# Level masks ahead on GpSimd, product copies on ScalarE, and one add for X and its transpose in the triangular inverse of an RWKV-7 mixer

## What is computed

```python
def wkv_scan(state0, r, kk, v, decay, b, k, reverse):
    def step(S, inp):
        r_t, kk_t, v_t, w_t, b_t, k_t = inp
        sa = jnp.einsum('bhvk,bhk->bhv', S, kk_t)
        S = S * w_t[:, :, None, :] - sa[..., None] * b_t[:, :, None, :] + v_t[..., None] * k_t[:, :, None, :]
        return S, jnp.einsum('bhvk,bhk->bhv', S, r_t)
    xs = tuple(jnp.moveaxis(t, 1, 0) for t in (r, kk, v, decay, b, k))
    S, ys = lax.scan(step, state0, xs, reverse=reverse)
    return S, jnp.moveaxis(ys, 0, 1)

def rwkv_mixer(z_lat, z_ctx, p, need_ctx):
    ...
    for d in range(2):
        reverse = d == 1
        s_ctx, yc = wkv_scan(s0, cx[0], cx[1], cx[2], *cx[4][d], reverse)
        _, yl = wkv_scan(s_ctx, lat[0], lat[1], lat[2], *lat[4][d], reverse)
```

## Time and profile before

| | us |
|---|---|
| median of 3 runs | 2557.57 (2556.31 to 2559.59) |
| the profiled execution, its time | 2553.7 |
| its span | 2551.6 |
| PE busy over the span | 2080.0 (82%) |
| DVE busy | 862.8 (34%) |
| POOL (GpSimd) busy | 377.2 (15%) |
| ACT (ScalarE) busy | 357.1 (14%) |

### The profile page before, as it was taken

The page is one execution under the profiler, slowest core; times in us unless marked ns, Lnnn a source line. Parts: engine busy times, 40 slices in busy tenths (PEclk is TensorE's granted clock), DMA queues, the critical chain, the costliest instruction groups (busy, mean ns, idle before and its releaser), DMA issues.

```text
span 2551.6 us, 40567 instructions
## 1 busy us (share of the span) xinstructions
PE 2080.0 (82%) x15579; PEld 1189.8 (47%) x15579; DVE 862.8 (34%) x1924; ACT 357.1 (14%) x724; POOL 377.2 (15%) x560
## 2 busy tenths in 40 slices
PE   3997897788857889889888588777857989999992
PEld 1332566664434444444444255566534444445441
DVE  3112267664671111111111734576472111111114
ACT  0111431111210001111010014111110101111110
POOL 0000000001101222222222110000002222222221
PEclk7998899999877999999999799898977999999996
DMA  9766010003007999999996920100207999999993
GB/s 370 255 245 215 0 42 2 11 2 121 25 27 264 386 385 390 377 364 373 373 376 261 346 92 1 42 2 11 105 17 303 402 381 386 392 378 373 371 359 134
DMA packets 150810, 571.69 MB, mean 224 GB/s; under 512 B 26735, under 2 KB 36847, under 8 KB 116768
## 3 DMA queue, kind: packets, MB, share of 16 engines
q1 hardware_dynamic: 125520, 530.03, 54.4%
q0 software_dynamic: 24576, 37.82, 4.3%
q10 hardware_dynamic: 592, 2.11, 0.2%
HBM read 569.75 MB, written 46.24 MB: 241 GB/s over the span
## 4 chain that ended last, share of the span: by engine, by line
PE 51%; DMA 28%; DVE 11%; issue 3%; ACT 3%; SPq 2%; POOL 1%; POOLq 0%; DVEq 0%; ACTq 0%
DMA arena<-in_exp_w_up_dram 24%; PE pb L1271 10%; PE pb L830 7%; PE pb L1290 3%; PE pb L1274 3%; PE pb L809 2%; PE pb L1013 2%; PE pb L777 2%; PE pb L1104 2%; PE pb L1221 1%; PE pb L1254 1%; PE pb L1105 1%; PE pb L898 1%; PE pb L864 1%; PE pb L909 1%
## 5 line engine op out<-in xcount | busy, mean ns | idle before, releaser
L1274 PE MATMUL pb<-arena 128*64 128x256 f32 x3072 | 357.1, 383 | 13.4 <-DMA arena<-in_exp_w_up_dram 12.8
L1271 PE MATMUL pb<-arena 128*128 128x512 f32 x512 | 268.1, 682 | 88.6 <-DMA arena<-in_exp_w_up_dram 86.2
L1274 PEld LDWEIGHTS pb<-arena 128*64 128x64 f32 x3072 | 216.9, 135 | 135.7 <-issue 36.5
L2112 DVE TENSOR_TENSOR arena<-arena,pb 128x128 f32<-128x128 f32 (+1 forms) x128 | 41.4, 323 | 681.5 <-ACT arena L1561 672.3
L809 PE MATMUL pb<-arena 128*128 128x128 f32 x1136 | 157.5, 283 | 94.8 <-DVE arena L1602 68.0
L1271 PEld LDWEIGHTS pb<-arena 128*128 128x128 f32 x512 | 109.0, 219 | 227.5 <-issue 227.4
L2155 POOL TENSOR_TENSOR arena<-arena 128x8 f32<-128x8 f32 (+1 forms) x41 | 69.8, 1701 | 906.4 <-DVE arena L1801 453.2
L809 PEld LDWEIGHTS pb<-arena 128*128 128x128 f32 x1136 | 128.5, 143 | 156.4 <-issue 89.5
L830 PE MATMUL pb<-arena 128*128 128x464 f32 (+3 forms) x480 | 186.8, 547 | 3.4 <-ACT arena L1371 3.4
L1290 PE MATMUL pb<-arena 128*64 128x512 f32 x768 | 186.0, 604 | 1.6 <-DVE arena L2118 1.6
L1561 ACT ACTIVATE arena<-pb 128x128 f32<-128x128 f32 (+1 forms) x128 | 39.3, 307 | 948.4 <-PE pb L1274 490.0
(11 more groups left out here) (296 smaller groups left out, 2679.6 us busy)
## 6 DMA issues: line engine op xcount, KB each, us to landing
arena<-in_exp_w_gate_dram SPq DMA_DIRECT2D x128, 1024.0 KB
arena<-in_exp_w_up_dram SPq DMA_DIRECT2D x128, 1024.0 KB
arena<-in_exp_w_down_dram SPq DMA_DIRECT2D x128, 1024.0 KB, 22.2
arena<-in_ada_w_dram SPq DMA_DIRECT2D x40, 1024.0 KB, 7.6
arena<-y_rows SPq DMA_DIRECT2D x36, 512.0 KB, 7.0
arena<-mod_rows SPq DMA_DIRECT2D x17, 512.0 KB, 6.6
arena<-in_ada_w_dram SPq DMA_DIRECT2D x4, 2048.0 KB, 14.0
arena<-in_w_in_dram SPq DMA_DIRECT2D x4, 1920.0 KB, 19.1
```

What stands on the lines that cost most here:

```text
L1271: last = mm(pb[:, 2 + j % 2, :], gT[:, j % 2, k, :], ring_gu[:, j, :, k, :], start=(k == 0), stop=(k == KD - 1))
L1274: last = mm(pb[f * FEW:(f + 1) * FEW, 2 + j % 2, 0:FF], gT_few[:, j % 2, k, :], ring_gu[:, j, :, k, f * P:(f + 1) * P], start=(k == 0), st ...
```

## The change

It moves the level mask from the product T to the matrix L. The mask of level k is constant on blocks, and X is block diagonal at that size, so masking L first gives the same T. GpSimd multiplies L by the masks of levels 2 to 5, two buffers in turn (`LM`), and T is then copied as it is from PSUM by ScalarE. Level 1 keeps its mask on DVE. X and X^T lie side by side (`XX`), their updates go to one PSUM bank, and DVE adds them in one operation of 512 columns, except in level 5. ScalarE also takes over the copy of M v, the negation and the gate's copy (L1828). The keys are no longer copied: the product reads them and M v through one strided view. ScalarE's program is written anew, so that its part of the front stands between these copies. The core of the diff, by engine:

```diff
 # PE
+                            if lv > 1 and d == 0:
+                                pe.wait_ge(R["lm_ready"], seen(R["lm_ready"]))
...
-                                    last = mm(pb[own, T1_BANK[d], h * C:(h + 1) * C], rb["LG"][own, d, h, 0, :], rb["X"][own, d, h, :],
-                                              start=True, stop=True)
+                                    L = rb["LG"][own, d, h, 0, :] if lv == 1 else rb["LM"][own, lv % 2, d, h, :]
+                                    last = mm(pb[own, T1_BANK[d], h * C:(h + 1) * C], L, rb["X"][own, d, h, :], start=True, stop=True)
...
-                                    last = mm(pb[own, 2 + d, h * C:(h + 1) * C], rb["T1"][own, d, h, :], rb["XT"][own, d, h, :],
-                                              start=True, stop=True)
+                                    to = pb[own, X_BANK[d], (RH + h) * C:(RH + h + 1) * C] if lv < 5 else pb[own, 2 + d, h * C:(h + 1) * C]
+                                    last = mm(to, rb["T1"][own, d, h, :], rb["XT"][own, d, h, :], start=True, stop=True)
...
-                                last = mm(pb[own, T1_BANK[d], h * P:(h + 1) * P], rb["XT"][own, d, h, :],
-                                          rb["KMV"][own, d, h].rearrange("p m n -> p (m n)"), start=True, stop=True)
+                                last = mm(pb[own, T1_BANK[d], h * P:(h + 1) * P], rb["XT"][own, d, h, :], k_and_kv(i, d, h, own),
+                                          start=True, stop=True)
 # ScalarE (the bodies of low_rank, low_rank_turned, squashed, decays, decays_before and arrays_turned are as before)
+                        ac(rb["g"][:, i, :], pb[:, 7, 8:8 + RW], ACT.Copy)
...
+                def t1_out(d):
+                    act.wait_ge(R["t1_sum"], seen(R["t1_sum"]))
+                    ac(rb["T1"][:, d].rearrange("p h t -> p (h t)"), pb[:, T1_BANK[d], 0:RH * C], ACT.Copy).then_inc(R["t1_ready"], 1)
+
+                def kv_out(d):
+                    act.wait_ge(R["mv_sum"], seen(R["mv_sum"]))
+                    ac(rb["KV"][:, d], pb[:, X_BANK[d], 0:RW], ACT.Copy).then_inc(R["kv_ready"], 1)
+
+                def nx_out(d):
+                    act.wait_ge(R["nx_sum"], seen(R["nx_sum"]))
+                    ac(rb["nX"][:, d].rearrange("p m h n -> p h m n"), pb[:, T1_BANK[d], :].rearrange("p (h m n) -> p h m n", h=RH, m=2),
+                       ACT.Copy, scale=-1.0).then_inc(R["nx_ready"], 1)
...
+                for i in range(NT):
+                    arrays_turned(i, 1)
+                    more = i + 1 < NT
+                    seen(R["t1_sum"], 2)
+                    for lv in range(2, 6):
+                        for d in range(2):
+                            t1_out(d)
+                        if more and lv < 5:
+                            (low_rank, low_rank_turned, squashed)[lv - 2](i + 1)
+                        if not more and lv == 2:
+                            turned_mix(1, 6, 0, 6)
+                    for d in range(2):
+                        kv_out(d)
+                    if more:
+                        decays(i + 1)
+                    for d in range(2):
+                        nx_out(d)
+                    if more:
+                        decays_before(i + 1)
+                        arrays_turned(i + 1, 0)
 # VectorE
-                        V.tensor_copy(rb["g"][:, i, :], pb[:, 7, 8:8 + RW])
...
-                        for d in range(2):
-                            dve.wait_ge(R["t1_sum"], seen(R["t1_sum"]))
-                            V.tensor_tensor(rb["T1"][:, d], pb[:, T1_BANK[d], 0:RH * C].rearrange("p (h t) -> p h t", h=RH),
-                                            levels[:, d, lv:lv + 1, :].broadcast_to([P, RH, C]), ALU.mult).then_inc(R["t1_ready"], 1)
-                        if lv == 5:
-                            for d in range(2):
-                                dve.wait_ge(R["mv_sum"], seen(R["mv_sum"]))
-                                V.tensor_copy(rb["KMV"][:, d, :, 0, :], heads(arr[:, 0, d, :]))
-                                V.tensor_copy(rb["KMV"][:, d, :, 1, :], heads(pb[:, X_BANK[d], 0:RW])).then_inc(R["kmv_ready"], 1)
+                        if lv == 1:
...
                         for d in range(2):
                             dve.wait_ge(R["x_sum"], seen(R["x_sum"]))
                             if lv < 5:
-                                V.tensor_tensor(rb["X"][:, d], pb[:, X_BANK[d], 0:RH * C].rearrange("p (h t) -> p h t", h=RH), rb["X"][:, d], ALU.add)
-                            V.tensor_tensor(rb["XT"][:, d], pb[:, 2 + d, 0:RH * C].rearrange("p (h t) -> p h t", h=RH), rb["XT"][:, d], ALU.add
-                                            ).then_inc(R["x_ready"], 1)
+                                both = rb["XX"][:, d].rearrange("p m h t -> p (m h t)")
+                                V.tensor_tensor(both, pb[:, X_BANK[d], :], both, ALU.add).then_inc(R["x_ready"], 1)
+                            else:
...
-                    for d in range(2):
-                        dve.wait_ge(R["nx_sum"], seen(R["nx_sum"]))
-                        V.tensor_scalar(rb["nX"][:, d].rearrange("p m h n -> p h m n"), pb[:, T1_BANK[d], :].rearrange("p (h m n) -> p h m n", h=RH, m=2),
-                                        -1.0, None, ALU.mult).then_inc(R["nx_ready"], 1)
...
-                dve.wait_ge(ms["iota_ready"], seen(ms["iota_ready"]))
 # GpSimd
-                roots(NT)
+                for i in range(NT):
+                    if i == 0:
+                        roots(1)
+                    for lv in range(2, 6):
+                        if lv == 2:
+                            pool.wait_ge(rs["mats_ready"], matrices + 2 * (i + 1))
+                            if i > 0:
+                                pool.wait_ge(rs["t1_sum"], products + 10 * i)
+                        elif lv > 3:
+                            pool.wait_ge(rs["t1_sum"], products + 10 * i + 2 * (lv - 2))
+                        nc.gpsimd.tensor_tensor(rb["LM"][:, lv % 2], rb["LG"][:, :, :, 0, :], levels[:, :, lv:lv + 1, :].broadcast_to([P, 2, RH, C]), ALU.mult
+                                                ).then_inc(rs["lm_ready"], 1)
+                        if lv == 3 and i + 1 < NT:
+                            roots(1)
```

More of the change, by code:

```diff
@@ L1495, in turned_mix @@
                        ).then_inc(mixT_ready, 1)
+                next(pooling)
+                low_rank(0)
+                next(pooling)
+                low_rank_turned(0)
+                for _ in range(2):
+                    next(pooling)
+                squashed(0)
+                for _ in range(2):
+                    next(pooling, None)
+                decays(0)
+                decays_before(0)
+                for _ in pooling:
+                    pass
+                seen(pool_sum, 2)
+                arrays_turned(0, 0)
+                for i in range(NT):
[18 more added lines that the diff above has]
+                        arrays_turned(i + 1, 0)
                 def squares(i):
```

76 lines of the change are left out of this document (41 added, 35 removed).

## The result

The changed kernel takes 2513.64 us (median of 4 runs, 2511.4 to 2514.83), the kernel before on the same chip 2556.94 (4 runs, 2553.5 to 2559.59). The ratio is 0.983, with a 95% interval of 0.9813 to 0.9847: 43.3 us faster. The forecast was 2528 with a range down to 2517, so the change did more than I said. The profiled execution has a span of 2512.1 us.

What follows compares the result with a forecast made beforehand. PE was taken to be held by the order of DVE's queue, not DVE's total. Profiled 2553.7 us less 26.8 (walk) and 3 (clock) gave 2523.9, or 2528 us beside the median; range 2518 to 2538, 2517 to 2543 over all cases.

Steps and rivals of the forecast that it cites:

- What bounds the kernel: Layer 0's RWKV tiles: the order of DVE's queue holds PE, 11.8 us of it waiting for the level mask.
- The walk through tile 0: Layer 0's tile 0, followed step by step: PE turns the arrays 4.6 us earlier, at 433.15 instead of 437.72.
- The new wait of 0.9 us: PE starts the low-rank product 0.9 us late, as ScalarE copies both directions of level 3 first.
- The masks: Four GpSimd multiplications of 128x512 a tile, taken at 1.2 us each and hidden.
- The 2.7 us: GpSimd's room in a tile: multiplications of up to 2.7 us each stay hidden.
- The sum of the walk: All tiles of both layers: 18.4 us from four like tiles, 2.8, 4.8, and 0.4 for each last tile; 26.8 us together.
- The last tiles: The last tile of each layer, without a front: 0.4 us gained each.
- two such drops fewer: Clock drops to 1.2 GHz behind PE's idle stretch at tile boundaries: two fewer at 1.5 us each, 3 us.
- all six 9: Upper case of the clock's term: all six drops to the lower clock gone, worth 9 us.
- the first: Rival: masks take 2.7 to 5 us each, or ScalarE's longer queue holds more than 0.9 us; 2542 us, chance 0.20.
- the second: Rival: GpSimd's masks become the bound, from 5.4 us each; at 8 us each 2630 us, slower; chance 0.04.
- the third: Rival: nothing changes, since PE's own work fills the time; 2557 us, chance 0.03.

Runs made afterwards that it cites:

- x3: Changed kernel with the copies of T put back on DVE in their old queue place, masks still on GpSimd: 2532.62 us, ratio 0.9906.
- x2: Changed kernel with the negation put back from ScalarE on DVE, ahead of the front's last piece: 2523.79 us, ratio 0.9864.
- x7: Kernel before with only the negation of a tile's last products moved from DVE to ScalarE: 2535.69 us, ratio 0.9916.
- x4: Changed kernel with the next tile's low-rank turn ahead of the copies of level 3 in ScalarE's queue: 2506.59 us, ratio 0.9808.
- x6b: Changed kernel with every mask computed twice by GpSimd, the second after the first has landed: 2524.47 us, ratio 0.987.
- x1: Kernel before with extra products that nobody reads, placed where PE would wait at a tile's end and start: 2544.22 us, ratio 0.9954.
- x9: Changed kernel with extra products that nobody reads, at the three places in a tile where PE would wait: 2518.77 us, ratio 0.9848.

## Why the prediction was wrong

**What bounds the kernel** was read rightly. x3 put the copies back into DVE's queue, and the wait of 11.8 us came back as 12.3. x2 and x7 moved the negation alone, and the wait for the last piece came and went with it.

**The walk through tile 0** held step by step, against its start of 399.10 before and 398.50 after:

| step | gained, predicted | gained, measured |
|---|---|---|
| third level's products | 1.7 | 1.71 |
| level 5's products | 2.5 | 2.77 |
| products with K and M v | 2.85 | 3.11 |
| closing products | 2.95 | 3.20 |
| turned arrays | 4.6 | 4.77 |

(Level 5's products stood at 421.94 and stand at 418.57.) The new wait of 0.9 us before the low-rank product is there with 0.80 us, behind ScalarE's L1470 as said, and x4 shows that it counts in full.

**The masks** take 1.28 us against the 1.2 assumed, and they are hidden. Those of levels 2 and 3 lie at 398.52 to 401.03, those of levels 4 and 5 at 412.43 to 414.94. The prediction put the length from which mask 5 reaches into the bias piece at 1.8 us; by the rows it is (415.90 - 412.43) / 2 = 1.7. The 2.7 us up to which I called the masks hidden is too generous, since x6b shows that VectorE is held there before any level waits for its mask.

**The sum of the walk**, 26.8 us, was nearly right. Tile 0 of layer 0, at a clock of 1.00 before and after, gave 4.70 us against 4.6; tile 1 of layer 1, at 0.93 and 0.92, gave 2.77 against 2.8. From x1, in which most of the clock is given back, to the changed kernel the stages fall by 14.2 + 15.3 = 29.5 us. The last tiles gave 0.1 and 0.3 us instead of 0.4 each.

**The step that failed** is the clock: "I count two such drops fewer, 2 x 1.5 = 3 us". It is a term of the right sign and mis-sized. The stages of x1 give it as 6.2 + 6.7 = 12.9 us, the medians as 9.5. What was wrong above all is the count. Cut into windows of 1 us, the view of stretches shows the kernel before at the lower level (1.2 GHz) for 61.4 us of both stages, in twelve places: 20.5 us in layer 0 and 40.9 in layer 1. The changed kernel spends 17.1 us there in two places, 6.8 in the chain of layer 0 and 10.2 across tiles 1 and 2 of layer 1; x1 spends 13.6. I had looked at the clock only in layer 0, while in layer 1 all three bodies were low too (0.90, 0.93, 0.87) and the last tile and the chain behind them (0.95, 0.76). So ten drops went and not two, and "all six 9" was no upper bound; 2518 as the low end rested on it. The price was nearer. The 1.5 us was the growth of PE's busy time in a window of 12 us; the body of tile 1, with 6.8 us at the lower level in one place, was 2.05 us longer than tile 0's, and that of tile 2, with 10.2 us in three places, 3.90. That is 0.30 and 0.38 us for each us at the lower level, and for the 44.3 us that went it makes an estimate of 13 to 17 us. (The 12.6 us in the expectation of x9 stop short of the end of layer 0's chain; with it they are 17.1.)

26.8 + 3 = 29.8 were forecast, 29.5 + 12.9 = 42.4 came in the stages of the traces, 43.3 by the medians. What is argued and not shown: the split is that of x1, which still has 13.6 us at the lower level and whose filling itself costs something (0.8 us in tile 1 of layer 1), and each side of it is one trace, so a few microseconds could stand on either side. With the 9.5 of the medians in place of the 12.9, the clock's term is still three times the 3 us of the forecast.

Of the rivals, the first (part of the gain lost to masks or ScalarE's queue) did not come, beyond the 0.80 us already in the sum; the second (masks as the bound) is far off at 1.28 us against 5.4; the third is refuted.

## What to carry to other kernels

In a chain of short steps between engines, read the granted clock of every repetition of the same body in all layers before you price a change, and take the difference between equal bodies at different clocks as the price: shortening a wait also shortens or removes the time at half clock behind it, and here that was some 10 to 13 of 42 us. When an operation on the path stands behind work for the next tile in one engine's queue, moving it to an engine that is idle then is worth the wait that it caused, even at the same length, less what new waits take back (the copies of T: 3.9 us of waits in tile 0, 2.87 us of the body); then look what stands ahead of it in the new queue (x4 gained another 0.8 to 1.2 us a tile from one reordering). An operation given to GpSimd should end before VectorE's next instruction with two SBUF inputs starts, not merely before its own result is wanted.

## What the runs showed of the hardware

A GpSimd multiplication of 128x512 from SBUF to SBUF took 1279 ns, as the mean of 32. Extra products on TensorE that nobody reads made a kernel 0.9954 times as long (0.9934 to 0.9973): it was at the lower clock for 13.6 us of two stages instead of 61.4; in the changed kernel the same products cost 0.7 to 1.1 us a body. A VectorE multiplication of 128x256 with both inputs in SBUF took 1.49 us instead of 0.42 beside a running GpSimd mask, ending 0.28 us after it, while the 128x1024 one behind it that reads PSUM kept its 1.23 us.
